# The first feed forward of a two-block decoder kernel: up and down slabs interleaved, and twelve down slabs by seven block products

## The reference, cut to what matters

```python
u = rmsnorm(h, norm_ff_g[l]) @ w1[l]          # [256, 1024] @ [1024, 4096]
h = h + jnp.square(jax.nn.relu(u)) @ w2[l]    # [256, 4096] @ [4096, 1024]
```

## Time and profile before

| | us |
|---|---|
| median of 3 runs | 884.16 (883.99 to 884.2) |
| the profiled execution | 884.08 |
| its span, first to last instruction | 882.2 |
| TensorE busy | 874.6 (99%) |
| VectorE busy | 647.6 (73%) |
| ScalarE busy | 502.4 (57%) |
| GpSimd busy | 117.9 (13%) |

### The profile page before, as it was taken

The page is one execution under the profiler, slowest core; times in us unless marked ns, Lnnn a source line. Parts: engine busy times, 40 slices in busy tenths (PEclk is TensorE's granted clock), DMA queues, the critical chain, the costliest instruction groups (busy, mean ns, idle before and its releaser), DMA issues.

```text
span 882.2 us, 15673 instructions
## 1 busy us (share of the span) xinstructions
PE 874.6 (99%) x6269; PEld 809.7 (92%) x6269; DVE 647.6 (73%) x881; ACT 502.4 (57%) x741; POOL 117.9 (13%) x136
## 2 busy tenths in 40 slices
PE   9999999999999999999999999999999999999997
PEld 9998988989989999888899989999998899999886
DVE  5887987656538887998775548978686788888643
ACT  7786655546547555545473356656634766666432
POOL 5561433000001000000142250001000100000000
PEclk9999999999999999999999999999999999999999
DMA  9969444354535666466556554354556386676641
GB/s 304 319 226 311 164 144 144 104 177 148 172 94 187 195 195 197 160 230 219 191 184 210 191 191 141 104 188 138 174 191 191 105 225 195 194 198 201 192 143 48
DMA packets 137399, 160.67 MB, mean 182 GB/s; under 512 B 4161, under 2 KB 113857, under 8 KB 137089
## 3 DMA queue, kind: packets, MB, share of 16 engines
q1 hardware_dynamic: 135280, 152.83, 54.1%
q0 software_dynamic: 1344, 6.03, 2.0%
q10 hardware_dynamic: 720, 1.06, 0.3%
HBM read 158.86 MB, written 1.05 MB: 181 GB/s over the span
## 4 chain that ended last, share of the span: by engine, by line
PE 98%; issue 1%; ACT 0%; DVE 0%; POOL 0%; DVEq 0%; POOLq 0%; ACTq 0%
PE tb L718 18%; PE tb L719 18%; PE tb L720 18%; PE acc L718 11%; PE acc L720 11%; PE acc L719 11%; PE acc L1043 1%; PE tb L1242 0%; PE tb L1122 0%; PE acc L1272 0%; PE tb L1140 0%; PE acc L1140 0%; PE acc L1290 0%; PE acc L1122 0%; PE tb L1241 0%
## 5 line engine op out<-in xcount | busy, mean ns | idle before, releaser
L1944 DVE TENSOR_TENSOR wlo<-raw,whi 128x2048 fp32r<-128x2048 f32 (+1 forms) x138 | 313.9, 2279 | 118.5 <-ACT whi L1389 117.9
L1389 ACT ACTIVATE whi<-raw 128x2048 fp32r<-128x2048 f32 (+1 forms) x138 | 261.4, 1896 | 140.6 <-PE acc L720 85.2
L718 PE MATMUL tb<-xhi,whi 128*128 128x256 f32 x1192 | 331.8, 278 | 0.2
L719 PE MATMUL tb<-xlo,whi 128*128 128x256 f32 x1192 | 329.5, 276 | 0.0
L720 PE MATMUL tb<-xhi,wlo 128*128 128x256 f32 x1192 | 329.5, 276 | 0.0
L718 PEld LDWEIGHTS tb<-xhi,whi 128*128 128x128 f32 x1192 | 224.1, 188 | 1.1 <-issue 1.0
L719 PEld LDWEIGHTS tb<-xlo,whi 128*128 128x128 f32 x1192 | 224.2, 188 | 0.1
L720 PEld LDWEIGHTS tb<-xhi,wlo 128*128 128x128 f32 x1192 | 224.0, 188 | 0.0
L720 PE MATMUL acc<-whi,xlo 128*128 128x512 f32 x112 | 44.0, 393 | 0.0
L718 PE MATMUL acc<-whi,xhi 128*128 128x512 f32 x112 | 43.8, 392 | 0.0
L719 PE MATMUL acc<-wlo,xhi 128*128 128x512 f32 x112 | 43.8, 391 | 0.0
(11 more groups left out here) (448 smaller groups left out, 1598.2 us busy)
## 6 DMA issues: line engine op xcount, KB each, us to landing
raw<-in_w_in SPq DMA_DIRECT2D x37, 1024.0 KB, 5.2
raw<-in_w SPq DMA_DIRECT2D x26, 1024.0 KB, 5.4
raw<-in_w_up SPq DMA_DIRECT2D x44, 512.0 KB, 5.0
raw<-in_w_down SPq DMA_DIRECT2D x22, 512.0 KB, 4.2
raw<-in_w_xkv SPq DMA_DIRECT2D x8, 1024.0 KB, 5.3
raw<-in_w_out SPq DMA_DIRECT2D x8, 1024.0 KB, 4.9
raw<-in_w SPq DMA_DIRECT2D x12, 512.0 KB, 4.5
raw<-in_w_mem_kv SPq DMA_DIRECT2D x4, 1024.0 KB, 5.2
```

The lines of the kernel that those rows point to most:

```text
L718: pe.matmul(o, a_hi, b_hi, start=start, stop=False)
L719: pe.matmul(o, a_hi, b_lo, start=False, stop=False)
L1389: act.activation(whi[:, n % RING, cut], raw[:, n % RING, cut], ACT.Copy).then_inc(hi_ready, 1)
L1944: dve.tensor_tensor(low(n)[:, cut], raw[:, n % RING, cut], whi[:, n % RING, cut].bitcast(F32), ALU.subtract).then_inc(lo_ready, 1)
```

## The change

The 32 slabs of the feed forward run in one list, `FIRST_FFN`: u is an up slab, s a down slab by seven products, n a plain one. Seven up slabs come first, then down and up slabs take turns. Twelve down slabs (0 to 6, 8, 10, 12, 14, 15) use seven products; the last of them, s15, is the third from the end, before n11 and n13. The hidden values are kept in seven places that are used again. Up slabs write banks `tb[0..3]`, `acc[0,0]` and `acc[1,1]`; before, they used three banks of `tb` in turn. ScalarE now does the square.

The weight forms are made in another way. For a seven-product slab n, SyncE loads two blocks (512 KB, `pair`) into one of two `pairs` buffers together with slab n-2; a DMA issued by GpSimd then adds two other blocks from memory onto them (512 KB, `accum_op`), and VectorE makes only two sums (`weight_sums`). The forms have buffers of their own, one set (`FORMS = 1`), instead of the room of `xhi` and `xlo`. At s15 ScalarE copies all four banks of `tb` to `pairs` (`kept`), TensorE's last slab waits for that copy, and `fold` reads the copy. `last_row_slab` no longer waits for the end of `fold`.

```diff
+HIDS = 7
+FORMS = 1
+SQUARES = 2
+FIRST_FFN = "u0 u1 u2 u3 u4 u5 u6 s0 u7 s1 u8 s2 u9 s3 u10 s4 u11 s5 u12 s6 u13 s8 u14 s10 u15 s12 n7 s14 n9 s15 n11 n13"
...
-    cols("w1", w["w1"], 0, 16)
-    rows("w2", w["w2"], 16)
+    first["w1"] = len(slabs)
+    for kind, j in ffn_order():
+        if kind == "u":
+            slabs.append(("T", w["w1"][:, j * 256:(j + 1) * 256].rearrange("(k p) c -> p k c", p=P), 8, 256, "act"))
+        else:
+            ap = w["w2"][j * 256:(j + 1) * 256, :].rearrange("(k p) c -> p k c", p=P)
+            slabs.append(("N", ap, 2, 1024, "dve" if len(slabs) == first["w1"] + 31 else None))
...
-    SEVEN = [first["w2"] + j for j in (1, 3, 5, 7, 9, 11)]
...
+    UP = {j: n0 + i for i, (kind, j) in enumerate(ORDER) if kind == "u"}
+    DOWN = {j: n0 + i for i, (kind, j) in enumerate(ORDER) if kind != "u"}
+    SEVEN = [n0 + i for i, (kind, j) in enumerate(ORDER) if kind == "s"]
+    PLAIN = [j for kind, j in ORDER if kind == "n"]
+    FFN_END = n0 + 31
...
+            def pair(n):
+                if n + 2 not in SEVEN:
+                    return
+                i = SEVEN.index(n + 2)
+                if i >= 2:
+                    sp.wait_ge(sev["lo"], 2 * i - 3)
+                sp.dma_start(pairs[:, i % 2, :, :], slabs[n + 2][1][:, :, 512:1024]).then_inc(raw_landed[n % RING], 16)
             def load(n, src=None, wait=None):
                 if n >= RING:
                     sp.wait_ge(lo_ready, n - RING + 1 if wait is None else wait)
                 if n - RING in SEVEN:
-                    sp.wait_ge(sev["lo"], 2 * SEVEN.index(n - RING) + 2)
+                    sp.wait_ge(sev["t"], SEVEN.index(n - RING) + 1)
                 _, ap, nk, c, _ = slabs[n]
                 if n in SEVEN:
                     forms = raw_forms(n)
-                    for c, slots in enumerate((slice(1, 3), slice(0, 4, 3))):
-                        sp.dma_start(forms[:, slots, :], ap[:, :, c * 512:c * 512 + 512]).then_inc(raw_landed[n % RING], 16)
+                    sp.dma_start(forms[:, 1:3, :], ap[:, :, 0:512]).then_inc(raw_landed[n % RING], 16)
+                    sp.dma_start(forms[:, 3, :], ap[:, 1, 512:1024]).then_inc(raw_landed[n % RING], 16)
+                    pair(n)
...
+            def add_blocks(n):
+                i = SEVEN.index(n)
+                pool.wait_ge(raw_landed[(n - 2) % RING], landed[n - 2])
+                if i >= 2:
+                    pool.wait_ge(sev["lo"], 2 * i - 3)
+                pool.dma_start(pairs[:, i % 2, :, :], slabs[n][1][:, 0, :].rearrange("p (a c) -> p a c", a=2),
+                               accum_op=ALU.add).then_inc(sev[f"acc{i % 2}"], 16)
+            add_blocks(SEVEN[0])
...
+            for n in SEVEN[1:]:
+                add_blocks(n)
...
+            for kind, j in ORDER[1:-1]:
+                if kind == "u":
+                    if j == 1:
+                        emptied(first["xo"] + 3)
+                    elif j not in (2, 3, 4, 5):
+                        emptied(UP[up_before(j)])
+                    t_slab(UP[j], XHI["h2"], XLO["h2"], None, whole=up_bank(j))
+                    continue
+                if DOWN[j] == SEVEN[0]:
+                    emptied(UP[5])
                 pe.wait_ge(ffn["lo"], j + 1)
-                if j == 1:
-                    emptied(first["w1"] + 15)
-                if first["w2"] + j in SEVEN:
-                    seven_slab(j, hid_hi, hid_lo)
+                if kind == "s":
+                    seven_slab(j)
                 else:
-                    row_slab(first["w2"] + j, hid_hi, hid_lo, 2 * j, 32)
-            pe.wait_ge(ffn["lo"], 16)
-            pe.wait_ge(sev["folded"], 1)
-            last_row_slab("x2", hid_hi, hid_lo, 30)
+                    plain_slab(j)
+            j = PLAIN[-1]
+            pe.wait_ge(sev["kept"], 1)
+            last_row_slab("x2", plain_hidden(hid_hi, j), plain_hidden(hid_lo, j), 0)
...
+            def relu_square(j):
+                act.wait_ge(slab_done, UP[j] + 1)
...
+                if j >= SQUARES:
+                    act.wait_ge(ffn["lo"], j - SQUARES + 1)
+                act.activation(sq[:, j % SQUARES, 0:512], ru[:, :], ACT.Square).then_inc(ffn["square"], 1)
+            def hidden_hi(j):
+                if seven(j):
+                    act.wait_ge(ffn["sq"], sum(seven(i) for i in range(j + 1)))
+                else:
+                    act.wait_ge(ffn["square"], j + 1)
+                if before[j] is not None:
+                    act.wait_ge(slab_done, DOWN[before[j]] + 1)
+                cut = hidden_place(j)
+                act.activation(hid_hi[:, cut], sq[:, j % SQUARES, 0:cut.stop - cut.start], ACT.Copy).then_inc(ffn["hi"], 1)
...
+            def form_hi(n, half):
                 i = SEVEN.index(n)
...
+                if i >= FORMS:
+                    act.wait_ge(slab_done, SEVEN[i - FORMS] + 1)
+                if half == 0:
+                    act.wait_ge(sev[f"acc{i % 2}"], 16 * (i // 2) + 16)
+                else:
+                    act.wait_ge(sev["t"], i + 1)
+                src, cut = form_places(n, half)
+                act.activation(forms_hi[:, i % FORMS, cut, :], src, ACT.Copy).then_inc(sev["hi"], 1)
...
+            for n, (kind, j) in enumerate(ORDER[:-1], first["w1"]):
+                if kind == "u":
+                    relu_square(j)
+                for m in split_after(n, True):
+                    form_hi(m, 0)
+                    form_hi(m, 1)
+                hi(n + RING)
+                if kind == "u":
+                    hidden_hi(j)
+                for m in split_after(n, False):
+                    form_hi(m, 0)
+                    form_hi(m, 1)
+                if n == SEVEN[-1]:
+                    act.wait_ge(slab_done, n + 1)
+                    act.activation(pairs[:, :, :, :].rearrange("p i s c -> p (i s) c"), tb[:, :, :], ACT.Copy)\
+                        .then_inc(sev["kept"], 1)
...
+            def hidden_sums(j):
+                a11, a21, a12, a22, s1, s2, s4 = (sq[:, j % SQUARES, s * P:s * P + P] for s in range(7))
+                dve.wait_ge(ffn["square"], j + 1)
+                link(dve.tensor_tensor(s1, a22, a21, ALU.subtract))
+                dve.tensor_tensor(a21, a11, a21, ALU.subtract)
+                link(dve.tensor_tensor(s2, s1, a11, ALU.add))
+                dve.tensor_tensor(s4, a12, s2, ALU.subtract).then_inc(ffn["sq"], 1)
+            def hidden_lo(j):
                 dve.wait_ge(ffn["hi"], j + 1)
...
+                cut = hidden_place(j)
+                dve.tensor_tensor(hid_lo[:, cut], sq[:, j % SQUARES, 0:cut.stop - cut.start], hid_hi[:, cut].bitcast(F32),
+                                  ALU.subtract).then_inc(ffn["lo"], 1)
...
+            def weight_sums(n):
                 i = SEVEN.index(n)
...
+                _, t1 = (pairs[:, i % 2, s, :] for s in (1, 0))
+                t2, t4 = rest[:, 0, :], rest[:, 1, :]
+                b21, b22 = (raw_forms(n)[:, s, :] for s in (2, 3))
+                dve.wait_ge(sev[f"acc{i % 2}"], 16 * (i // 2) + 16)
+                dve.wait_ge(raw_landed[n % RING], landed[n])
+                if i:
+                    dve.wait_ge(sev["lo"], 2 * i)
+                link(dve.tensor_tensor(t2, t1, b22, ALU.add))
+                dve.tensor_tensor(t4, t2, b21, ALU.add).then_inc(sev["t"], 1)
+            def form_lo(n, half):
+                i = SEVEN.index(n)
+                src, cut = form_places(n, half)
+                dve.wait_ge(sev["hi"], 2 * i + half + 1)
+                dve.tensor_tensor(forms_lo[:, i % FORMS, cut, :], src, forms_hi[:, i % FORMS, cut, :].bitcast(F32),
+                                  ALU.subtract).then_inc(sev["lo"], 1)
...
+                dve.wait_ge(nrm["rs"], RS["h2"] + 2)
                 dve.wait_ge(sev["kept"], 1)
...
+                p1, p5, p6, p7 = (pairs[:, s // 2, s % 2, :] for s in range(4))
+                dve.tensor_tensor(p6, p1, p6, ALU.subtract)
+                link(add(p1, 0, 0))
+                dve.scalar_tensor_tensor(p1, p6, -1.0, p5, ALU.mult, ALU.subtract)
+                link(dve.tensor_tensor(p7, p6, p7, ALU.add))
+                add(p1, 0, 1)
+                add(p7, 1, 0)
+                link(dve.scalar_tensor_tensor(p5, p7, -1.0, p5, ALU.mult, ALU.subtract))
+                link(add(p5, 1, 1))
+            for n, (kind, j) in enumerate(ORDER[:-2], first["w1"]):
+                if kind == "u" and seven(j):
+                    hidden_sums(j)
+                for m in split_after(n, True):
+                    form_lo(m, 0)
+                    form_lo(m, 1)
+                lo(n + RING)
+                if n + RING in SEVEN:
+                    weight_sums(n + RING)
+                if kind == "u":
+                    hidden_lo(j)
+                for m in split_after(n, False):
+                    form_lo(m, 0)
+                    form_lo(m, 1)
+                if n == SEVEN[-1]:
                     fold()
...
```

(2 more changed lines are left out.)

248 lines of the change are left out of this document (97 added, 151 removed).

## The result

| | before | after |
|---|---|---|
| median, us | 884.12 (883.99 to 884.35, 6 runs) | 888.26 (886.66 to 889.72, 6 runs) |
| the profiled execution | 884.08 | 889.72 |
| its span | 882.2 | 888.0 |
| TensorE busy | 874.6 (99%) | 873.9 (98%) |

The changed kernel takes 1.0048 times as long, 95% interval 1.0038 to 1.0059: 4.1 us slower, where I forecast 1.4 us faster, within a range that ended at 885.8. Its runs also spread over 3.1 us, those of before over 0.4.

A forecast was written before the change was run, and what follows sets the result against it. TensorE, busy 99% of the span, was taken to bound the kernel. The terms -4.08 + 0 + 0 + 2.7 = -1.4 us, off the median 884.16, gave 882.8 us, range 881.0 to 885.8, counted as no change.

The forecast's parts named there:

- What bounds the kernel: Whole kernel: TensorE is busy 99% of the span, so only fewer matmuls and new gaps between them move the time.
- Part 1: Feed forward: six more slabs by seven products remove 18 matmuls of 0.2267 us, -4.08 us.
- Part 2: Alternating up and seven-product slabs: VectorE needs about 9.1 of 10.2 us and keeps up; 0, with 0 to 1.0 us.
- Part 3: DMAs of the alternating slabs: bandwidth suffices and landings fit their buffers' loop; cost 0.
- The latency has a loop of its own: `pairs` buffers: each serves every 20.4 us, leaving 16 for two landings of 10.6, at worst 14.9; cost 0.
- Bandwidth, the other half of Part 3: Alternating slabs: 2.88 MB in 10.2 us, 282 GB/s, against 372 sustained at the kernel's start; plain bandwidth is there.
- My guess that an add may count like a transfer more: Adding DMA: if reading its target counts like a transfer, demand is 334 GB/s, still under 372.
- Part 4: Near the end: TensorE waits 2.7 us (2.3 to 3.1) for fold and residual in the last down slab.
- X: Start of the fold's time count: the first matmul of n11, right after s15.
- the clock: Rival, 8%: the new 2.7 us gap lowers the clock, losing up to 3.1 us; up to 885.9, middle 884.4.
- The late adding DMA: Rival, 16%: two landings over 16 us make TensorE wait in every second seven-product slab; at 17 us +5, 887.8.
- its own range: The forecast's range without rivals: 882.4 to 883.8 us, from fold waits of 2.3 to 3.1 and up to 1.0 of Part 2.

The follow-up runs named there:

- the early order: Changed kernel with the pair's load on its own semaphore and the first seven-product slab one up slab earlier: 880.46 us, ratio 0.9964 to the kernel before.
- eleven slabs: Changed kernel with the pair's load on its own semaphore and n15 plain in place of s15: 880.99 us, ratio 0.9968 to the kernel before.
- own semaphore: Changed kernel with the pair's load counting on its own semaphore, not that of the raw slab two places ahead: 884.19 us, ratio 1.0004 to the kernel before.
- the own semaphore and the filler: Changed kernel with the pair's load on its own semaphore and 20 unused transposes in TensorE's idle time ahead of the last down slab: 882.84 us, ratio 0.9987.
- Cutting every second one: Changed kernel with the pair's load on its own semaphore for six of twelve seven-product slabs, the others still shared: 884.63 us, ratio 1.0009 to the kernel before.

## Why the prediction was wrong, point by point

**What bounds the kernel**: held. TensorE's pace is 0.227 us in both kernels, and only gaps and the clock moved the time.

**Part 1, -4.08 us**: held. 18 matmuls fewer, and the two kernels without gaps show the gain: 884.1 - 4.1 = 880.0, the early order took 880.5; and with eleven slabs, so 3 matmuls more, 880.7 against 881.0.

**Part 2, VectorE keeps up**: held. Once the circle is open it is busy for 47.8 of 52 us (308 to 360, own semaphore), 0.92, where I had 9.1 of 10.2, 0.89, and TensorE doesn't wait for it. Seen by the releasers alone the changed kernel says the opposite: all gaps there are released by VectorE's `forms_lo` and `wlo`. It was late because ScalarE was, and ScalarE because of a DMA; an engine named as releaser is the last link, and need not be the cause. Its own share shows it: 42.2 of 52 us in 308 to 360, so it had room.

**Part 3, the DMAs at 0**: this is the step that failed, and in it the passage that begins "The latency has a loop of its own" and ends with a cost of 0. The runs put 4.2 us in its place (888.38 against 884.19). The loop that I counted, one buffer of `pairs` in 20.4 us with 16 us for two landings, is real and holds: 4.2 + 8.2 = 12.4 us, more than the 10.6 that I took, less than 14.9. But I counted only the loop that the data make. The semaphores made a second one, of half the period, in which 3.3 to 3.7 us are left for one landing that takes 4.2 at the median and 6.35 in the turn above. It stood in the diff, in the term `16 * (n + 2 in SEVEN)` of `landed` and in the `then_inc` of `pair`. With the question who waits on this semaphore, and for what else, it could have been worked out from rows of before: 4.5 us for 512 KB in an uncrowded stage and 6.7 of work by the earlier trace rows (a high part of 1536 columns at three quarters of 1.92, then 1.76, 1.38, 0.9 and 1.2) are 11.2 for a turn of 10.2. The Trainium skill ("DMA: Bandwidth & Descriptors", Why a DMA increments its semaphore by 16 and not by 1) asks for one semaphore per in-flight slot, so that no reader takes one transfer's count for another's. Here the count waits for all transfers, and no reader is early; what the runs add is that the sharing can cost time, 4.2 us.

Bandwidth, the other half of Part 3, held: the DMA share is 0.95 and 0.97 with the own semaphore (308 to 360 and 360 to 400 us), 0.97 and 0.98 in the early order, without a gap of TensorE. My guess that an add may count like a transfer more was near: see below.

**Part 4, the fold, 2.7 us**: held. The bracket has 2.45; counted from start to start, as the forecast was, it is 2.6. With X at 430.37 its steps can be laid beside the timelines of ScalarE and VectorE (they answer to the earlier trace rows):

```profile
430.63 1.92 ACT L1487 ACTIVATE whi<-raw 128x2048 fp32r<-128x2048 f32 x1 [2.84 <-PE acc L800]
432.45 1.87 ACT L1841 ACTIVATE pairs<-tb 128x2048 f32<-128x2048 f32 x1
```

```profile
432.58 2.29 DVE L2054 TENSOR_TENSOR wlo<-raw,whi 128x2048 fp32r<-128x2048 f32 x1 [2.19 <-ACT whi L1487]
434.79 0.68 DVE L2462 TENSOR_TENSOR pairs<-pairs 128x512 f32<-128x512 f32 x1
...
440.34 1.41 DVE L2094 SCALAR_TENSOR_TENSOR h<-acc,rs,h 128x512 f32<-128x512 f32 x2
```

The high part is at X + 0.26 as forecast, the low part at X + 2.21 (2.2), the fold at X + 4.42 (4.4), its end at X + 9.97 (10.1). The copy of four banks took 1.87 us where the line through one and two banks gave 2.13.

**The rivals.** I held the clock to be an alternative to the forecast, at 8%. It came on top of it, since the gap that lowers it is part of the forecast: a gap forecast at 2.7 us with a chance of a lower clock belonged into the sum. Its price of 1.6 us lies between 0 and the 3.1 that I had as an end. The late adding DMA would have given about the measured time, 887.8, and much of its signature (gaps in seven-product slabs, VectorE late), and it was still the wrong mechanism: the own semaphore takes the loss away and leaves this DMA as slow as it was, at 7.9 us. A rival that ends near the measured time isn't thereby shown.

**The range.** It was added up wrongly at one place: "its own range is 882.4 to 883.8" takes 3.1 us of the fold's wait and 1.0 of Part 2, and both together end at 884.2. That changes neither the range as a whole (881.0 to 885.8) nor what failed.

Taken together: 884.1 - 4.1 + 2.6 is 882.6, and the kernel with the own semaphore and the filler, which has these two terms and no others, took 882.8. What the sum lacked was 4.2 us for the circle and 1.3 to 1.6 for the clock.

## What to carry to other kernels

Where a DMA is put on a semaphore that something else waits for, go once around each circle of waits that this closes: add up the work and the landing in one turn and hold it against the period in which it must turn. A circle that is 0.9 us too long cost nothing here for the first few turns and then in most turns, and it showed in the profile as short gaps released by an innocent engine. Cutting every link took the 4.2 us away, and cutting every second one all but 0.4 of them at the median. And where a forecast contains a new idle gap of TensorE, price the lower clock behind it in the sum, and look whether the step can be moved ahead by one slab, which here gave back the gap and the clock together.
